# Feed-forward up slots of a float32 transformer kernel: one load of the high weights for a 512 column operand

## The reference, cut to what matters

```
def swiglu(h, w1, w3, w2):
    return (jax.nn.silu(h @ w1) * (h @ w3)) @ w2
```

## Time and profile before

| | us |
|---|---|
| median of 3 runs (1312.68 to 1316.29) | 1315.99 |
| the profiled execution | 1313.43 |
| its span, first to last instruction | 1311.6 |
| TensorE matmul busy | 1283.5 |
| TensorE weight load busy | 1233.1 |
| GpSimd busy | 1007.0 |
| ScalarE busy | 686.3 |
| VectorE busy | 634.5 |

### The profile page before, as it was taken

How to read it: one execution, slowest core, us unless ns; L and a number is a source line. 1 busy time by engine, 2 the same in 40 slices (tenths; PEclk the granted TensorE clock), 3 DMA queues, 4 the chain that set the end, 5 groups by cost and what they waited for, 6 DMA issues and landing times.

```text
span 1311.6 us, 27700 instructions
## 1 busy us (share of the span) xinstructions
PE 1283.5 (98%) x10992; PEld 1233.1 (94%) x10992; DVE 634.5 (48%) x1152; ACT 686.3 (52%) x954; POOL 1007.0 (77%) x794
## 2 busy tenths in 40 slices
PE   8999999999999999999999999999999999999999
PEld 7889999999988989999998978999999899999998
DVE  8995655555536756555555673211113545311112
ACT  8834643444667665444366475434436666544342
POOL 5227988888775669888878894988887766988885
PEclk9999999999999999999999999999999999999999
DMA  6316765455544325545545432554554433555530
GB/s 272 130 33 242 205 223 193 170 182 192 171 156 157 131 101 198 190 169 186 192 161 181 171 133 97 193 188 169 188 192 141 157 129 129 193 179 178 189 128 32
DMA packets 33879, 217.07 MB, mean 165 GB/s; under 512 B 3683, under 2 KB 7428, under 8 KB 8196
## 3 DMA queue, kind: packets, MB, share of 16 engines
q1 hardware_dynamic: 30096, 211.14, 45.4%
q10 hardware_dynamic: 3700, 4.75, 1.5%
HBM read 213.26 MB, written 2.62 MB: 165 GB/s over the span
## 4 chain that ended last, share of the span: by engine, by line
PE 80%; DVE 11%; ACT 5%; issue 2%; POOL 1%; DMA 0%; DVEq 0%; ACTq 0%; POOLq 0%
PE up L1621 18%; PE up L1622 17%; PE up L1623 17%; PE acc L1621 7%; PE acc L1623 7%; PE acc L1622 7%; DVE opnd L1023 2%; ACT w_hi L531 1%; PE up L1756 1%; DVE s_work L1163 1%; ACT opnd L692 1%; PE side L1629 1%; DVE s_work L1172 1%; PE acc L1991 0%; DVE mix L1028 0%
## 5 line engine op out<-in xcount | busy, mean ns | idle before, releaser
L422 POOL TENSOR_TENSOR w_lo<-ring,w_hi 128x512 fp32r<-128x512 f32 x740 | 945.5, 1312 | 237.5 <-ACT w_hi L531 215.8
L1621 PE MATMUL up<-opnd,w_hi 128*128 128x256 f32 x1984 | 569.4, 287 | 4.5 <-DVE opnd L1023 1.5
L1622 PE MATMUL up<-opnd,w_lo 128*128 128x256 f32 x1984 | 561.3, 283 | 0.0
L1623 PE MATMUL up<-opnd,w_hi 128*128 128x256 f32 x1984 | 561.2, 283 | 0.0
L531 ACT ACTIVATE w_hi<-ring 128x2048 fp32r<-128x2048 f32 x185 | 353.1, 1910 | 257.8 <-PE up L1623 202.2
L1621 PEld LDWEIGHTS up<-opnd,w_hi 128*128 128x128 f32 x1984 | 380.3, 192 | 16.9 <-issue 12.4
L1622 PEld LDWEIGHTS up<-opnd,w_lo 128*128 128x128 f32 x1984 | 380.4, 192 | 1.2 <-issue 1.0
L1623 PEld LDWEIGHTS up<-opnd,w_hi 128*128 128x128 f32 x1984 | 380.4, 192 | 0.0
L1621 PE MATMUL acc<-opnd,w_hi 128*128 128x256 f32 x816 | 232.1, 284 | 1.2 <-DVE x L1271 1.2
L1622 PE MATMUL acc<-opnd,w_lo 128*128 128x256 f32 x816 | 230.9, 283 | 0.0
L1623 PE MATMUL acc<-opnd,w_hi 128*128 128x256 f32 x816 | 230.9, 283 | 0.0
(11 more groups left out here) (307 smaller groups left out, 1432.3 us busy)
## 6 DMA issues: line engine op xcount, KB each, us to landing
ring<-in_stream SPq DMA_DIRECT2D x197, 1024.0 KB, 4.8
bias_rows<-mix ACTq DMA_DIRECT2D x1, 1536.0 KB
x<-in_x SPq DMA_DIRECT2D x1, 1024.0 KB, 5.8
mix<-in_s_b SPq DMA_DIRECT2D x1, 1024.0 KB, 7.8
mix<-in_s_c SPq DMA_DIRECT2D x1, 1024.0 KB, 11.7
mix<-bias_rows ACTq DMA_DIRECT2D x1, 1024.0 KB, 5.6
out_x<-x SPq DMA_DIRECT2D x8, 128.0 KB, 1.7
mix<-in_p ACTq DMA_DIRECT2D x2, 256.0 KB, 3.3
```

The lines of the kernel that those rows point to most:

```text
L422: ins = nc.gpsimd.tensor_tensor(w_l[:, cols], ring[:, r, cols], w_h[:, cols].bitcast(f32), ALU.subtract)
L1621: MM(o, l_hi, r_hi, start=start, stop=False, skip_group_check=True)
L1622: MM(o, l_lo, r_hi, start=False, stop=False, skip_group_check=True)
L1623: return MM(o, l_hi, r_lo, start=False, stop=stop, skip_group_check=True)
```

## The change

Of the 22 up slots of each layer, the last 20 (all but the first two) become wide slots. In a wide slot TensorE loads a block of high weights once and streams high and low operand side by side, 512 columns, into a whole bank: the low operand's product lies in columns 256 to 511. The low weights' product with the high operand is added to columns 0 to 255. So there are 32 loads and 32 matmuls (16 of 512 columns, 16 of 256) where there were 48 and 48 of 256. The gate now fills one bank, and `gate_ps` is raised after it; then the value fills the other bank, and `mm_done` is raised. VectorE, for each of the two, copies columns 256 to 511 out of PSUM, adds them to columns 0 to 255 there, and multiplies by `rstd`, which frees that bank; each of these waits for the one before. The gate's three come before the wait for the value.

```diff
@@ stages
-    _u += {"ffn": 2 * STEPS, "ple": 4}.get(_name[:3], _n)
+    _u += {"ffn": 2 + 4 * (STEPS - 1), "ple": 4}.get(_name[:3], _n)
@@ operands
+        def hi_and_lo(name, k):
+            return opnd[SET[name]][:, :, k]
@@ VectorE
+            def wide_over_rms(dst, u, t):
+
+                step(V.tensor_copy(f_h[:, t], up[u][:, 1]))
+                step(V.tensor_tensor(up[u][:, 0], up[u][:, 0], f_h[:, t], ALU.add))
+                c.up_and_wait(V.tensor_tensor(dst, up[u][:, 0], rstd[:], ALU.mult), "up_free")
@@ VectorE, tile
-                    dve.wait_ge(sem("mm_done"), s + k + 1 if i is None else i * 6 + (s + k + 1))
+                    wide = n >= 2
+                    if wide:
+                        c.wait("gate_ps")
+                    else:
+                        dve.wait_ge(sem("mm_done"), s + k + 1)
                     if conv:
-                        over_rms(f_u[:, 0:2, 2:258], u)
+                        if not wide:
+                            over_rms(f_u[:, 0:2, 2:258], u)
                         for t, o in ((0, gate_ps), (1, val_ps)):
+                            if wide:
+                                if t:
+                                    dve.wait_ge(sem("mm_done"), s + k + 1 if i is None else i * 6 + (s + k + 1))
+                                wide_over_rms(f_u[:, t, 2:258], (up0 + t) % 2, t)
...
+                    elif wide:
+                        wide_over_rms(gate_ps, up0 % 2, 0)
+                        c.tell("g_ready")
+                        dve.wait_ge(sem("mm_done"), s + k + 1 if i is None else i * 6 + (s + k + 1))
+                        wide_over_rms(val_ps, (up0 + 1) % 2, 1)
                     else:
                         over_rms(side[:, :, 0:T], u)
@@ TensorE, bank
-                    pe.wait_ge(sem("up_free"), u - 1 if i is None else i * 4 + (u - 1))
+                    pe.wait_ge(sem("up_free"), u - 1 if i is None else i * 8 + (u - 1))
@@ TensorE
+            def wide_slot(name, s, i=None):
+
+                slot_ready(s, i)
+                w_h, w_l = weights_hi(s), weights_lo(s)
+                for m in range(2):
+                    o = bank(i)
+                    for k in range(KT):
+                        w = slice((2 * k + m) * P, (2 * k + m + 1) * P)
+                        MM(o[:], w_h[:, w], hi_and_lo(name, k), start=(k == 0), stop=False, skip_group_check=True)
+                        ins = MM(o[:, 0], w_l[:, w], hi(name)[:, k], start=False, stop=(k == KT - 1),
+                                 skip_group_check=True)
+                    c.up(ins, ("gate_ps", "mm_done")[m])
@@ TensorE, ffn
-                up_slot(name, S + 2)
-                up_slot(name, S + 3)
+                wide_slot(name, S + 2)
+                wide_slot(name, S + 3)
...
-                        up_slot(name, S + 8 + k, i)
-                        up_slot(name, S + 9 + k, i)
+                        wide_slot(name, S + 8 + k, i)
+                        wide_slot(name, S + 9 + k, i)
```

More of the change, by code:

```diff
@@ L1261, in ffn @@
                 with dve.Fori(0, 4) as i:
-                    c.enter(i, **(dict(dve_step=20, up_free=4, g_ready=4, gated=4, h_raw=4, h_hi=4, h_ready=4) if conv
-                                  else dict(up_free=4, g_ready=4, gated=4, h_raw=4, h_hi=4, h_ready=4)))
+                    c.enter(i, **(dict(dve_step=36, gate_ps=4, up_free=8, g_ready=4, gated=4, h_raw=4, h_hi=4, h_ready=4)
+                                  if conv else dict(dve_step=16, gate_ps=4, up_free=8, g_ready=4, gated=4, h_raw=4, h_hi=4, h_ready=4)))
                     for j in (3, 4):
@@ L1921, in ffn @@
                 down(S + 4, 0, first=True)
-                up_slot(name, S + 5)
-                up_slot(name, S + 6)
+                wide_slot(name, S + 5)
+                wide_slot(name, S + 6)
                 down(S + 7, 1)
                 with pe.Fori(0, 4) as i:
-                    c.enter(i, h_ready=4, mm_done=6)
+                    c.enter(i, h_ready=4, mm_done=6, gate_ps=4)
                     for k in (0, 3):
-                        up_slot(name, S + 8 + k, i)
-                        up_slot(name, S + 9 + k, i)
+                        wide_slot(name, S + 8 + k, i)
+                        wide_slot(name, S + 9 + k, i)
                         down(S + 10 + k, k // 3, i=i)
                     c.leave(4)
-                used[0] += 3 * 4
+                used[0] += 3 * 8
                 last_down_slot(S + 32, 0)
```

## The result

| | before | after |
|---|---|---|
| median of 7 runs each, us | 1314.31 | 1318.94 |
| lowest to highest | 1312.68 to 1316.29 | 1317.22 to 1321.86 |
| profiled execution (span) | 1313.43 (1311.6) | 1317.22 (1315.4) |

The ratio is 1.0037 with a 95% interval of 1.0025 to 1.0049: 4.6 us slower, 3.8 between the two profiled executions. The median lies in the stated range, and the sign is that of the forecast, but the forecast was +10: less than half of it came. The prediction called anything over 4 us, or over 1320, slower: the measured median is 4.6 over the 1314.31 of seven runs and still under 1320, so it stands at the edge between its "within" (0.20) and its "slower" (0.70).

What follows compares the result with a forecast made beforehand. TensorE, busy 98% of the span, was the bound, with VectorE taking over in ffn0 and ffn1's loops. Those layers' +14.4 us and ffn2 and ffn3's -4.4 gave +10.0, 1326.0 us against median 1315.99; range 1313 to 1339.

Steps and rivals of the forecast that it cites:

- within: Outcome of no change that a measurement can tell, about 4 us either way: 1312 to 1320 us, chance 0.20.
- TensorE's part: Wide slots on TensorE: a 512 + 256 column pair costs 353 ns, a slot 5.65 us, 0.11 less than before.
- Rival A: Weight loads set TensorE's pace: a pair at 334 ns, -5.2 us, 1310.8 us; chance 0.12.
- Rival C: Merged load on TensorE gains nothing, 512 columns running as two of 256: +15.4 us, 1331.4 us; chance 0.10.
- VectorE becomes the bound of the convolution layers' loops: ffn0 and ffn1, 8 loop steps: two VectorE tiles of 8.85 us take 17.70 us, over TensorE's 17.06.
- the sign that the prediction gave for it: Profile of ffn0 and ffn1 loops: VectorE never waiting for TensorE, a 17.7 us step, TensorE idle 0.6 us a step.
- The first stall: Start of ffn0 and ffn1: TensorE waits 2.5 us for slot S+3's gate bank, 2.7 with the value bank.
- the wait at the end: Last down slot of ffn0 and ffn1: TensorE waits about 2 us on the last tile's h_ready.
- In the loop over steps a dependent instruction follows 0.12 us behind: VectorE's hand-over price in the ffn0 and ffn1 loops, used in the 8.85 us tile; unrolled steps 0.03 to 0.04.
- Rival B: VectorE stays under the step in ffn0 and ffn1, tile under 8.53 us: -3.4 us, 1312.6 us; chance 0.10.
- Rival D: Dearer VectorE hand-overs in the convolution loops, near 0.27 us, tile about 9.3 us: +24.4 us, 1340.4 us; chance 0.08.

## Why the prediction was right or wrong

- *TensorE's part:* right. A pair was put at 353 ns and took 353; ffn2 and ffn3 were put at -2.2 each and gained 2.14 and 2.13. Taking the float32r rows of line 2245 and not the float32 ones was the right choice. Rival A (loads set the pace) fell: PEld went from 40 us to 36 and the slot by 2%. Rival C (no gain) fell by the same rows, 353 ns and not 360. The Trainium skill's page Perfetto Trace Analysis (Identifying the Most-Contended Engine) spoke for A; the measurement decides against it here. That page gives no time, so the prediction went too far where it said that its rule gives A's. The Trainium skill's page TensorE: Matmul & The Clock Gate (Back-to-back issue gap) would have given 216 ns for 512 columns; 0.236 us was measured.
- *VectorE becomes the bound of the convolution layers' loops:* right, shown by the added copy (the loop 6.5 and 6.6 us longer) and by the two kernels that take work from VectorE. But two loop tiles took 17.2 us against TensorE's 17.06, not 17.7, and the sign that the prediction gave for it did not show in ffn0: TensorE has no idle 0.6 us in each step (it is busy 39.96 of 40 us); the lateness gathers and comes out at the last down slot.
- *The first stall:* right, put at 2.5, measured 2.67 us; *the wait at the end:* there, 1.65 us in ffn0 and 1.86 in ffn1, where about 2 was put.
- **The step that failed** is "In the loop over steps a dependent instruction follows 0.12 us behind". It was read between lines 1242 and 1251, where register work is done behind a wait, and applied to four hand-overs inside the halves and to the one between tiles, where it is 0.04: 5 x 0.08 = 0.4 us a tile, 8.85 put and 8.45 measured. In ffn1 the hand-over between tiles was 0.12, as put, and the tile 8.54.

  Against it stands the loop's turn, which I had put at nothing: 0.54 us, three times within the 16 tiles, so 1.5 over the 0.04 of the other hand-overs. Four gaps in front of line 1260 in ffn0, one a turn, were 0.25 to 0.50 us where the others are 0.14, 0.7 together; what makes them is open.

  From the start of the first loop tile to the end of the last, ffn0 took 137.7 us where 141.6 was put, 3.9 less, and ffn1 138.6, 3.0 less. The layer as a whole was put at +7.2 and gave +3.64 and +4.45. The forecast of +10.0 is 6.2 over the +3.8 of the two profiles: 6.3 too much in these two layers, 0.1 too little in the other two.

  Rows for 0.04 were in the trace, between dependent instructions of the unrolled steps; none in the loop was without register work.
- *Rival B's point of decision* was 8.53 us a tile. The tile was 8.45, but the turns and the longer gaps bring the mean of the 16 to 8.60: just over the point. That near it, 0.1 us a tile is 1.6 us a layer, and my range for the tile (8.7 to 9.1) lay wholly above what was measured. That the median is inside the stated range is luck in part: the range reached down to 1313 by way of a pair of 343 ns and a tile of 8.7 us, and neither was there. Rival D (dearer hand-overs) fell: 0.04 and not near 0.27 between copy, add and product.
- *The clock* was costed at nothing by not being named. The profiled execution had it at 1.00 throughout the work, as before; five of the seven runs did not, and the median is 1.7 us over the profiled execution. The +3.8 of the profiles and the +4.6 of the medians differ in part by that, in part by the runs of before (their median 0.9 over the profiled one).

## What to carry to other kernels

A merged weight load was worth 7 ns here, 2% of the slot and not a third, although the loads' row was busy without a gap: price it from rows of the same data type at both widths. When work moves to a second engine, sum that engine's dependent chain per step, with each hand-over read at a place that has the same register work, and compare it with the step; here 0.1 us a tile is 1.6 us a layer. Moving 0.42 us of copy to an engine with time to spare turned +0.4% into -0.2%, and starting two slots later as well made it -0.6%. Start a layer's new scheme only when the engine that must release its banks has caught up.

## What the runs showed of the hardware that was not expected

**In some executions the clock falls behind a stall of TensorE.** Windows around the first stall of the kernel with early wide slots and ScalarE's copies:

```profile
150.00:153.80 3.80, 3.80 (x23) 3.12 (x21) 3.55 (x8) 1.31 (x2) 3.80 (x4) 1.00 0.65 95
153.90:156.10 2.20, 0.01 (x1) 0.01 (x1) 1.57 (x5) 1.97 (x4) 2.19 (x2) 1.00 0.82 245
156.20:159.60 3.40, 3.40 (x11) 2.92 (x12) 3.19 (x7) 1.05 (x2) 2.66 (x3) 0.50 0.86 313
159.60:163.00 3.40, 3.40 (x20) 2.94 (x20) 2.71 (x7) 0.66 (x2) 2.35 (x2) 0.99 0.61 253
```

TensorE had been busy to 153.9, was idle for 2.2 us, and then had the granted clock at 0.50 (1.2 GHz) for 3.4 us: 11 matmuls, against 20 in the 3.4 us behind. It costs about 1.7 us. In the kernel with VectorE's added copy it stands behind the wait at ffn0's end too, and behind the same two in ffn1:

```profile
331.40:334.00 2.60, 0.00 (x0) 0.00 (x0) 1.80 (x4) 0.93 (x2) 1.18 (x1) 1.00 0.37 88
334.10:337.40 3.30, 3.30 (x15) 3.30 (x16) 1.06 (x3) 3.27 (x5) 2.07 (x2) 0.50 0.72 288
```

Shorter stalls have a fall close behind them too: 1.75 us at the end of ffn1 (wide slots from the fifth on) and 1.69 us at 47.4 (the kernel with ScalarE's copies). Not every stall does it: the kernel without the low half has stalls of 1.74 and 1.75 us in these layers and no fall behind them, and the changed kernel's own profile has two of 2.67 and 2.68 and none. Nor do all falls belong to the change: six of the ten profiles of the experiments have one at 48 to 52 us, ahead of the first feed-forward layer. Over the executions the mean clock tells the number of falls. With early wide slots and ScalarE's copies, the runs at 1.000 took 1308.9 to 1309.8 us and those at 0.996 or 0.997 took 1312.5 to 1314.8. The changed kernel's runs at 1.000 took 1317.2 and 1317.8, those at 0.995 and 0.996 1319.7 to 1321.9. The Trainium skill (TensorE: Matmul & The Clock Gate, HAM oscillation) warns that an idle TensorE loses its clock and is slow for a while after; these falls, behind gaps of 2.2 and 2.6 us, agree with that, and the stall of 2.67 us without one shows that the length of a gap alone does not decide it here.

**VectorE's add of two SBUF operands is slow beside GpSimd:** 0.42 us alone, up to 1.56 beside GpSimd's subtractions, which went from 1.29 to 1.35 us. With an operand in PSUM it took 0.43 always. This is why the form with an instruction more was the faster one.

**A loop's turn** costs VectorE 0.54 us where it is the bound; in the kernel before, it was hidden in a wait for TensorE of 4.6 us.

**A hand-over between dependent VectorE instructions** costs 0.03 to 0.04 us, in a hardware loop too, and 0.12 with one register operation of 40 ns in it: 75 and 28 gaps in the loop of ffn0, with no exception.
